# A diffusion backbone block on one core: transform table loaded earlier, value folds and inverse split by parity, filter envelopes on VectorE, more filler matmuls

## The chip, the core and the metric

The kernel runs on one core of a Trainium2 chip. The metric is the time on the device of one launch, in microseconds. A core has TensorE (PE: matmuls, with weight loads PEld beside them), VectorE (DVE), ScalarE (ACT), GpSimd (POOL) and SyncE (SP), which here only issues transfers. Each engine works through its own list in order and waits on semaphores that others raise.

## The reference

Two layers over 1024 latent tokens of width 1024, with 256 context tokens, all in float32. Layer 0 mixes with gated linear attention (GLA) in 4 heads and, in 512 channels, with a bidirectional Hyena convolution; layer 1 mixes with a gated short convolution. Each layer ends in a mixture of experts: top group of 4, then the top 2 of its 8 experts. The change touches the Hyena convolution:

```python
t = jnp.linspace(0.0, 1.0, L)[:, None]
hh = jnp.sin(f2 * (jnp.sin(f1 * (z @ w1 + b1)) @ w2 + b2)) @ w3
window = jnp.exp(-t * jnp.abs(deltas)[None])
hh = hh.reshape(L, 2, HY_WIDTH) * window[:, None]      # h_fwd, h_bwd
U = jnp.fft.rfft(u, n=2*L, axis=1)
K = jnp.fft.rfft(h_fwd, n=2*L, axis=0) + jnp.conj(jnp.fft.rfft(h_bwd, n=2*L, axis=0))
y = jnp.fft.irfft(U * K[None], n=2*L, axis=1)[:, :L]
out = x0 * (y + u * skip)                              # u = v * x1
```

## The kernel before

All of SBUF that is worked on is one arena with tiles laid over each other in time; the eight banks of PSUM are reused likewise. The order of the work on every engine is written out by hand, and waits are counts of semaphores.

**The start.** TensorE makes the modulation vectors from four slabs of weights of 2 MB, then GLA projections and heads; the Hyena projections are put between the heads' steps. `fold` turns finished modulation rows to columns.

**The Hyena part**, in the order of TensorE:
1. `hyena_transposes`: the value tile VX (channels by time) is turned to time by channels in PSUM, and ScalarE copies it into VTM (L965), one half for each parity `par` of time. `vtm_ready` counts the copies. VX is VectorE's product L2022.
2. `residue` (L1386): the values times the transform table DFT, for two groups g of frequencies, four pairs i = (par, fn) each, two banks (s = 0, 1) a pair. ScalarE copies the second bank to USECOND (L974), VectorE writes sum and difference into USUM[g] (L2040, L2043). `butterfly` counts these folds. USUM[1] lies over VTM.
3. Filter rows (L1417): 8 tiles t of filter values for both directions from the hidden layer HH2 (64 partitions) and W3H. ScalarE copies one bank to FTMP (L979); VectorE makes HSUM and HDIF (L2051, L2052), then multiplies HSUM with the envelope WIN (L2056) while GpSimd multiplies HDIF (L715). After every second t come `gate_part` matmuls (L1171), which spread the gates over the partitions, and a `gate_row` copy.
4. `filter_spectrum` (L1396): four blocks kt of the filters' transform, from HSUM and HDIF. For each block VectorE makes sums (L2072, L2073) and complex products with USUM into YF (L2080 to L2089); after each second block four pair additions (L2100) and four pair differences (L2103).
5. `inverse` (L1440): the inverse transform, half g = 0 from the first two blocks and g = 1 from the others; each accumulates `part(c, par, g)` for 4 channel tiles c and 2 parities of time in bank 2c + par. VectorE adds the skip and multiplies with x0 (L2113, L2116).
6. `mix_and_route` (L1473 and on): output projection, residual, norm, router, tables of the experts' rows.

**SyncE's queue** issues in this order: envelope table, (wait: last Hyena projection, hidden filter layer, VX finished) filter hidden layer, W3H, DFT (4 MB, over the projections' input U), (wait: envelope products) IDFT, output weights, x again for the residual (after the inverse's last matmul).

**Experts** take 24 passes of 128 rows in each layer: `turn` transposes gathered rows, `pass_up` twice (L1608), `pass_down` (L1632). The final rows are combined after the last pass has been scattered, and `ov_left` is raised by all five engines before the next part.

**Fillers.** `spare(n, b)` puts n matmuls of constants into a bank that nobody reads:

```python
def spare(n, b):
    for _ in range(n):
        nc.tensor.matmul(bank(b)[:, 0:256], ident, cst[:, 0:256], start=True, stop=True)
```

Each is two instructions at L1115.

## Time and profile before

| what | value |
|---|---|
| runs | 2656.6, 2666.64, 2668.95 us; median 2666.64 |
| profiled execution | 2666.26 us, its span 2664.3 us |
| mean clock granted to TensorE | 0.956 |
| busy, share of the span | PE 92%, PEld 42%, DVE 38%, ACT 12%, POOL 6% |

A start time counts from the begin of the span. An entry such as `564.00 30.53 PE L1386 ... x64 [14.93 <-DMA ...]` is a run of 64 instructions of line 1386 that began at 564.00, ended 30.53 us later, and before which the engine had been idle for 14.93 us until the named transfer landed. A float32 matmul shows as two instructions. A granted clock of 1.00 is 2.4 GHz, 0.50 is 1.2 GHz; a stretch between holds both.

### The profile page before, as it was taken

What the parts mean: (1) busy time and instruction counts of PE and PEld (TensorE: products, weight loads), DVE (VectorE), ACT (ScalarE), POOL (GpSimd) and SP (SyncE); (2) the same over time, 40 slices, a digit from 0 to 9 for tenths busy, and PEclk for the clock granted to TensorE, in tenths of its full rate; (3) what the DMA queues carried; (4) which work ended last, traced back from release to release, by engine and by line L of the source; (5) the groups of instructions that cost most, each with busy time, mean ns of one, the idle gap of its engine ahead of it and who ended that gap; (6) DMA issues with size and microseconds to landing.
All of it is one profiled execution on the core that took longest, in us unless ns stands there. A gap on an engine that the chain in (4) does not pass through costs nothing. (4 is left out here: it accounts for less than half of the span.)

```text
span 2664.3 us, 32938 instructions
## 1 busy us (share of the span) xinstructions
PE 2459.2 (92%) x14399; PEld 1109.7 (42%) x14400; DVE 1018.8 (38%) x2030; ACT 332.4 (12%) x648; POOL 152.8 (6%) x171
## 2 busy tenths in 40 slices
PE   5999998969999899999999799999999999999991
PEld 3455444535555533333333544444555333333330
DVE  2787477726846422222121411011464222222214
ACT  2211233320011100000000410000111000000001
POOL 2000000001000000000000000000000000000000
PEclk9999999986999899999999899999998999999995
DMA  9575001010120799999997701010007999999975
GB/s 338 182 259 196 16 24 30 34 71 32 63 87 32 284 349 397 388 390 395 381 369 304 236 24 47 24 55 32 24 32 294 373 390 384 385 393 383 395 280 214
DMA packets 121869, 572.04 MB, mean 215 GB/s; under 512 B 11744, under 2 KB 48808, under 8 KB 94713
## 3 DMA queue, kind: packets, MB, share of 16 engines
q1 hardware_dynamic: 104328, 526.47, 51.6%
q0 software_dynamic: 17312, 43.16, 4.1%
q8 instruction: 115, 1.88, 0.3%
q10 hardware_dynamic: 80, 0.26, 0.0%
q14 instruction: 34, 0.27, 0.0%
HBM read 548.61 MB, written 38.01 MB: 220 GB/s over the span
## 5 line engine op out<-in xcount | busy, mean ns | idle before, releaser
L1608 PE MATMUL ps<-arena 128*32 128x512 f32 x6144 | 693.2, 604 | 28.5 <-DMA arena<-in_ex_w_dram 27.9
L1608 PEld LDWEIGHTS ps<-arena 128*32 128x32 f32 x6144 | 200.2, 112 | 453.5 <-issue 452.2
L1632 PE MATMUL ps<-arena 128*32 128x512 f32 x3072 | 343.4, 599 | 8.9 <-DMA arena<-in_ex_w_dram 8.8
L1710 PE MATMUL ps<-arena 128*128 128x512 f32 x768 | 330.4, 593 | 4.5 <-ACT arena L1003 4.5
L2315 DVE TENSOR_SCALAR arena<-ps,gain_x,mod 128x128 f32<-128x128 f32 x384 | 126.8, 403 | 373.4 <-PE ps L1593 373.4
L1473 PE MATMUL ps<-arena 128*128 128x512 f32 x512 | 226.6, 597 | 2.9 <-DVE arena L2116 1.6
L1710 PEld LDWEIGHTS ps<-arena 128*128 128x128 f32 x768 | 146.0, 190 | 186.3 <-issue 186.3
L1632 PEld LDWEIGHTS ps<-arena 128*32 128x32 f32 x3072 | 108.4, 111 | 234.7 <-issue 234.7
L2347 DVE SCALAR_TENSOR_TENSOR arena<-ps,arena,gates 128x512 f32<-128x512 f32 x96 | 72.1, 751 | 263.9 <-PE ps L1632 263.9
L1284 PE MATMUL ps<-arena 128*128 128x512 f32 x384 | 167.3, 594 | 0.7 <-issue 0.7
L2323 DVE TENSOR_TENSOR arena<-arena,ps 128x512 f32<-128x512 f32 x48 | 52.6, 1095 | 276.0 <-PE ps L1608 276.0
L1473 PEld LDWEIGHTS ps<-arena 128*128 128x128 f32 x512 | 95.3, 191 | 112.6 <-issue 108.8
L1063 ACT ACTIVATE arena<-ps 128x512 f32<-128x512 f32 x48 | 28.7, 597 | 743.9 <-PE ps L1575 743.9
L2449 DVE TENSOR_TENSOR arena<-arena,ps 128x1024 f32<-128x1024 f32 x8 | 9.8, 1220 | 281.9 <-PE ps L1710 281.9
L1284 PEld LDWEIGHTS ps<-arena 128*128 128x128 f32 x384 | 72.2, 191 | 87.9 <-issue 87.4
L1862 DVE SCALAR_TENSOR_TENSOR arena<-arena,silu_c 128x512 f32<-128x512 f32 x120 | 90.2, 752 | 4.3
L733 POOL DMA_INDIRECT expert_rows<-arena x48 | 48.1, 1001 | 753.0 <-DVE arena L2347 753.0
L1115 PE MATMUL ps<-constants 128*128 128x256 f32 x270 | 73.0, 424 | 0.0
L1061 ACT ACTIVATE arena<-ps 128x512 f32<-128x512 f32 x48 | 28.7, 597 | 351.9 <-PE ps L1608 351.9
L1208 PE MATMUL ps<-arena 128*128 128x512 f32 x160 | 70.1, 595 | 0.0
L723 POOL DMA_INDIRECT arena<-normed_rows,arena x48 | 48.6, 1013 | 371.4 <-PE ps L1593 299.7
L1247 PE MATMUL ps<-arena 128*128 128x512 f32 (+1 forms) x160 | 63.3, 553 | 0.0
(287 smaller groups left out, 2078.8 us busy)
## 6 DMA issues: line engine op xcount, KB each, us to landing
arena<-in_ex_w_dram SPq DMA_DIRECT2D x192, 2048.0 KB, 11.9
arena<-in_mod_w_dram SPq DMA_DIRECT2D x24, 2048.0 KB, 8.7
arena<-expert_rows SPq DMA_DIRECT2D x16, 1024.0 KB, 8.6
arena<-in_od_w_in_dram SPq DMA_DIRECT2D x24, 512.0 KB, 6.4
arena<-in_x_dram SPq DMA_DIRECT2D x2, 4096.0 KB, 15.0
normed_rows<-arena POOLq DMA_DIRECT2D x16, 512.0 KB, 2.9
arena<-in_ev_w_in_dram SPq DMA_DIRECT2D x3, 2048.0 KB, 13.0
arena<-in_ev_w_in_dram SPq DMA_DIRECT2D x12, 512.0 KB, 4.2
```

The source lines that it names most:

```text
L1115: nc.tensor.matmul(bank(b)[:, 0:256], ident, cst[:, 0:256], start=True, stop=True)
L1208: ins = nc.tensor.matmul(bank((2, 3, 6)[i % 3]), u_cols(i, j), w[:, j], start=j == 0, stop=j == KC - 1)
L1247: ins = nc.tensor.matmul(bank(s % 4)[:, 0:n], wqk[:, j, c0:c0 + P], u_part(part, j), start=j == 0, stop=j == KC - 1)
L1284: ins = nc.tensor.matmul(bank(6 + half), HYP[n % 3][:, j], u_part(half, j), start=j == 0, stop=j == KC - 1)
L1473: ins = nc.tensor.matmul(bank(m % 4), mixed[:, j, i * P:(i + 1) * P], slab(first[half], KC, 512)[:, j], start=j == 0, stop=j == KC - 1)
L1608: ins = nc.tensor.matmul(bank(2 + m)[c:c + n], x[:, j, c:c + n], w_slot(e % 2, m, KC, FE)[:, j], start=j == 0, stop=j == KC - 1)
L1632: ins = nc.tensor.matmul(bank(5 + half)[c:c + n], HT[:, j * P + c:j * P + c + n], w_slot(e % 2, 2, FC, D)[:, j, half * 512:(half + 1) * 51 ...
L1710: ins = nc.tensor.matmul(bank(2 * k + half), slab(L1_IN + c, 3, KC, P)[:, k, j], u_part(half, j), start=j == 0, stop=j == KC - 1)
L1862: link(V.scalar_tensor_tensor(out=acc, in0=w[:, j], scalar=silu_c[:, j, 0:1], in1=acc, op0=ALU.mult, op1=ALU.add))
L2315: ins = V.tensor_scalar(XT[:, b, j * P:(j + 1) * P], bank(j // 4)[:, (j % 4) * P:(j % 4 + 1) * P], gain_x[:, 2 * l + 1, j:j + 1], mod[:, l ...
L2323: return V.tensor_tensor(HS.rearrange("t (c p) -> t p c", p=P), SL.rearrange("t (p c) -> t p c", c=FC), bank(3).rearrange("t (p c) -> t p ...
L2347: V.scalar_tensor_tensor(out=YS[:, b, cs], in0=bank(5 + half), scalar=PASS_GATE[:, p:p + 1], in1=gates[:, 1, cs], op0=ALU.mult, op1=ALU.mu ...
```

## The change

- The DFT table's issue moves ahead of the waits for the filter's hidden layer and VX, and of the two filter loads; it waits only for the last Hyena projection.
- The residues' banks are renumbered (2i + s instead of (2i + 4) mod 8 + s), so the filter rows' first banks are those of i = 0 and 1. USUM[1] is laid out so that the folds of i = 0 and 1 fall on the half of VTM for parity 0; they wait for 12 residues instead of 16. The first filter rows wait for 10 and 12 folds instead of 14 and 16.
- GpSimd's eight products of HDIF with the envelope go to VectorE, behind those of HSUM.
- In the inverse the parity becomes the outer loop and the channel tile the inner one. The pair folds are split into those for even and those for odd outputs, and the matmuls of a parity wait only for theirs. The skip and mix follow in the same order.
- Fillers: three more behind each of the first three modulation slabs; two and one more in the tail of each layer's router; nine more ahead of the first expert transposes and six more ahead of the last pass down, in each layer; ten new ones ahead of the short convolution.

```diff
 HSUM, HDIF = at(4096, 2 * KT, HW), at(30720, 2 * KT, HW)
-USUM = [at(0, 8, HW), at(34816, 8, HW)]
+USUM = [at(0, 8, HW), at(34816, 2, 4, HW)]
+
+def usum(g, q):
+    return USUM[1][:, q % 2, q // 2] if g else USUM[0][:, q]
+
 PTMP = [at(20480, 2, HW), at(47104, 2, HW)]
...
     sp.wait_ge(hy_mm, 6 * HC)
+    sp.dma_start(at(12288, 8192), a["dft"]).then_inc(tables_in, 16)
     sp.wait_ge(flt_in, 64)
...
     sp.dma_start(W3H[0:HID], a["hy_w3"][0]).then_inc(flt_in, 16)
-    sp.dma_start(at(12288, 8192), a["dft"]).then_inc(tables_in, 16)
...
     pool.wait_ge(tables_in, 32)
-    for t in range(2 * KT):
-        pool.wait_ge(dif_ready, t + 1)
-        nc.gpsimd.tensor_tensor(HDIF[:, t], HDIF[:, t], WIN[:, t], ALU.mult).then_inc(filt_win, 1)
...
                 act.wait_ge(butterfly, 2 * (i + 1))
-            nc.scalar.activation(USECOND[:, i], bank((2 * i + 4) % 8 + 1), ACT.Copy).then_inc(uk_ready, 1)
+            nc.scalar.activation(USECOND[:, i], bank(2 * i + 1), ACT.Copy).then_inc(uk_ready, 1)
     for t in range(2 * KT):
...
             if n < NMOD - 1:
-                spare(4, 7)
+                spare(7, 7)
             if n == 2:
...
             pe.wait_ge(butterfly, 2 * (i + 1))
-        elif i == 2:
+        elif i == 0:
             pe.wait_ge(omix_ready, 2 * HEADS)
         for tc in (2 * s, 2 * s + 1):
-            ins = nc.tensor.matmul(bank((2 * i + 4) % 8 + s), DFT[:, 2 * g, fn, par, tc * P:(tc + 1) * P], VTM[:, par, tc],
+            ins = nc.tensor.matmul(bank(2 * i + s), DFT[:, 2 * g, fn, par, tc * P:(tc + 1) * P], VTM[:, par, tc],
                                    start=tc == 2 * s, stop=tc == 2 * s + 1)
...
             else:
-                pe.wait_ge(butterfly, 14 + 2 * t)
+                pe.wait_ge(butterfly, 10 + 2 * t)
             for k in range(2):
...
         for g in range(2):
-            pe.wait_ge(butterfly, folds_before(2 * g + 2))
-            for c in range(HC):
-                for par in range(2):
+            for par in range(2):
+                pe.wait_ge(butterfly, folds_before(2 * g + 2) - 4 + 4 * par)
+                for c in range(HC):
                     if g == 0:
...
         turn_rows(TT - 1)
-        spare(4, 2)
+        spare(6, 2)
         places(TT - 2)
-        spare(1, 2)
+        spare(2, 2)
         logits(TT - 1)
...
         table_of_gates(l)
-        spare(2, 2)
+        spare(11, 2)
         turn(0)
...
             turn_hidden(p)
-        spare(12, 0)
+        spare(18, 0)
         pass_down(NP - 1)
...
+        spare(10, 0)
         pe.wait_ge(ov_left, 5)
...
     for g in range(2):
-        u = USUM[g]
         for i, (plus, minus, turned) in enumerate(((0, 4, 0), (2, 6, 1), (1, 7, 0), (3, 5, 0))):
-            dve.wait_ge(dft_mm, 16 if g else 2 * (i + 1))
+            dve.wait_ge(dft_mm, (12 if i < 2 else 16) if g else 2 * (i + 1))
             dve.wait_ge(uk_ready, 4 * g + i + 1)
-            first, second = bank((2 * i + 4) % 8), USECOND[:, i]
-            V.tensor_tensor(u[:, plus], first, second, ALU.add).then_inc(butterfly, 1)
+            first, second = bank(2 * i), USECOND[:, i]
+            V.tensor_tensor(usum(g, plus), first, second, ALU.add).then_inc(butterfly, 1)
             if turned:
                 first, second = second, first
-            V.tensor_tensor(u[:, minus], first, second, ALU.subtract).then_inc(butterfly, 1)
+            V.tensor_tensor(usum(g, minus), first, second, ALU.subtract).then_inc(butterfly, 1)
...
         V.tensor_tensor(HSUM[:, t], HSUM[:, t], WIN[:, t], ALU.mult).then_inc(filt_win, 1)
+        V.tensor_tensor(HDIF[:, t], HDIF[:, t], WIN[:, t], ALU.mult).then_inc(filt_win, 1)
         if t % 2:
...
             for fn in range(2):
-                a, b = USUM[g][:, 4 * half + 2 * fn], USUM[g][:, 4 * half + 2 * fn + 1]
+                a, b = usum(g, 4 * half + 2 * fn), usum(g, 4 * half + 2 * fn + 1)
                 V.tensor_tensor(a, a, b, ALU.add).then_inc(butterfly, 1)
...
         dve.wait_ge(butterfly, folds_before(kt) + 4)
-        u, y = USUM[kt // 2][:, 4 * (kt % 2):4 * (kt % 2) + 4], YF[:, kt]
+        u, y = [usum(kt // 2, 4 * (kt % 2) + q) for q in range(4)], YF[:, kt]
         if kt:
...
             t0, t1 = (PTMP[row // 2][:, q] for q in range(2))
-            step(V.tensor_tensor(y[:, row + 1], u[:, 0], w[:, second], ALU.mult))
-            step(V.tensor_tensor(y[:, row], u[:, 2], w[:, 2 - second], ALU.mult))
-            n = step(V.tensor_tensor(t0, u[:, 1], w[:, second + 1], ALU.mult))
-            step(V.tensor_tensor(t1, u[:, 3], w[:, 3 - second], ALU.mult))
+            step(V.tensor_tensor(y[:, row + 1], u[0], w[:, second], ALU.mult))
+            step(V.tensor_tensor(y[:, row], u[2], w[:, 2 - second], ALU.mult))
+            n = step(V.tensor_tensor(t0, u[1], w[:, second + 1], ALU.mult))
+            step(V.tensor_tensor(t1, u[3], w[:, 3 - second], ALU.mult))
             settle(n)
...
             pairs = ((y[:, 0], z[:, 0], 1), (y[:, 2], z[:, 2], -1), (y[:, 1], z[:, 3], 1), (y[:, 3], z[:, 1], 1))
-            for p, q, sign in pairs:
-                V.tensor_tensor(p, p, q, ALU.add if sign > 0 else ALU.subtract).then_inc(butterfly, 1)
-            for n, (p, q, sign) in enumerate(pairs):
-                dve.wait_ge(butterfly, folds_before(kt) + 4 + n + 1)
-                V.scalar_tensor_tensor(out=q, in0=q, scalar=-2.0 * sign, in1=p, op0=ALU.mult, op1=ALU.add)\
-                    .then_inc(butterfly, 1)
-    for c in range(HC):
-        for par in range(2):
-            n = 2 * c + par
-            dve.wait_ge(idft_mm, n + 1)
+            for m in (0, 2):
+                for p, q, sign in pairs[m:m + 2]:
+                    V.tensor_tensor(p, p, q, ALU.add if sign > 0 else ALU.subtract).then_inc(butterfly, 1)
+                for n, (p, q, sign) in enumerate(pairs[m:m + 2]):
+                    dve.wait_ge(butterfly, folds_before(kt) + 4 + 2 * m + n + 1)
+                    V.scalar_tensor_tensor(out=q, in0=q, scalar=-2.0 * sign, in1=p, op0=ALU.mult, op1=ALU.add)\
+                        .then_inc(butterfly, 1)
+    for par in range(2):
+        for c in range(HC):
+            n, m = 2 * c + par, HC * par + c
+            dve.wait_ge(idft_mm, m + 1)
             sl = slice(par, SEQ - 1 + par, 2)
-            tmp = CTMP[:, n % 2]
-            if c:
-                dve.wait_ge(hmix_ready, n - 1)
+            tmp = CTMP[:, m % 2]
+            if m >= 2:
+                dve.wait_ge(hmix_ready, m - 1)
             link(V.scalar_tensor_tensor(out=tmp, in0=VX[:, c, sl],
```

## Rows read from the trace of the kernel before

**Rows 1.** The page's slices: the clock granted to TensorE, in tenths (40 equal slices).
```profile
PEclk9999999986999899999999899999998999999995
```

**Rows 2.** Timeline of TensorE, Hyena part (start, us, engine, line, operation; in brackets the idle before).
```profile
524.50 1.45 PE L1284 MATMUL ps<-arena 128*128 128x512 f32 x3
...
564.00 30.53 PE L1386 MATMUL ps<-arena 128*128 128x512 f32 x64 [14.93 <-DMA arena<-in_dft_dram]
598.38 7.18 PE L1417 MATMUL ps<-arena 64*128 64x512 f32 x8 [3.86 <-DVE arena L2043]
605.50 3.67 PE L1171 MATMUL ps<-constants,mod 128*128 128x64 f32 x16
...
641.70 56.71 PE L1396 MATMUL ps<-arena 128*128 128x512 f32 x128 [0.29 <-DVE arena L2056]
...
717.79 16.78 PE L1440 MATMUL ps<-arena 128*128 128x256 f32 x64 [5.56 <-DVE arena L2103]
736.13 20.87 PE L1473 MATMUL ps<-arena 128*128 128x512 f32 x48 [1.57 <-DVE arena L2116]
```

**Rows 3.** Timelines of ScalarE and of SyncE's queue, before the transform table lands.
```profile
549.10 0.60 ACT L965 ACTIVATE arena<-ps 128x512 f32<-128x512 f32 x1 [0.26 <-PE ps L1369]
...
548.29 0.58 SPq L609 DMA_DIRECT2D arena<-in_dft_dram  x1
```

**Rows 4.** Stretches: busy us (x instructions) of each engine; near the end TensorE's granted clock.
```profile
564.00:570.00 6.00, 6.00 (x8) 2.59 (x9) 0.00 (x0) 0.00 (x0) 0.00 (x0) 0.53 0.00 0
570.00:594.50 24.50, 24.50 (x58) 10.57 (x56) 5.15 (x8) 4.18 (x7) 0.00 (x0) 1.00 0.00 1
...
598.40:641.40 43.00, 43.00 (x96) 24.07 (x96) 25.87 (x29) 4.78 (x8) 10.60 (x8) 0.50 0.00 0
641.70:645.00 3.30, 3.30 (x4) 1.51 (x5) 3.23 (x6) 0.00 (x0) 0.00 (x0) 0.53 0.72 194
...
717.80:723.40 5.60, 5.60 (x14) 4.50 (x15) 1.44 (x2) 0.00 (x0) 0.00 (x0) 0.51 0.37 138
```

**Rows 5.** Timeline of VectorE in the filter rows: the envelope products of t = 0 and 1.
```profile
604.30 0.69 DVE L2056 TENSOR_TENSOR arena<-arena 128x512 f32<-128x512 f32 x1
...
607.65 1.75 DVE L2056 TENSOR_TENSOR arena<-arena 128x512 f32<-128x512 f32 x1
```

**Rows 6.** Timeline of VectorE during the spectrum and the inverse.
```profile
671.61 0.69 DVE L2072 TENSOR_TENSOR arena<-ps,arena 128x512 f32<-128x512 f32 x1 [1.24 <-ACT arena L985]
...
702.04 0.68 DVE L2073 TENSOR_TENSOR arena<-ps,arena 128x512 f32<-128x512 f32 x1
...
712.83 2.50 DVE L2100 TENSOR_TENSOR arena<-arena 128x512 f32<-128x512 f32 x4
```

**Rows 7.** Timeline of TensorE at the places of the fillers.
```profile
39.49 1.92 PE L1143 MATMUL ps<-arena 128*32 128x512 f32 x16 [0.69 <-DMA arena<-in_mod_w_dram]
...
880.98 1.95 PE L1496 MATMUL ps<-w_router,arena 128*128 128x36 f32 x16 [0.61 <-DVE arena L2192]
...
899.64 2.06 PE L1115 MATMUL ps<-constants 128*128 128x256 f32 x4
904.25 1.97 PE L1593 MATMUL ps<-constants,arena 128*128 128x128 f32 x8 [2.56 <-DMA arena<-normed_rows,arena]
...
1456.93 7.05 PE L1632 MATMUL ps<-arena 128*32 128x512 f32 x64
...
1464.40 5.35 PE L1115 MATMUL ps<-constants 128*128 128x256 f32 x24
1474.01 8.77 PE L1632 MATMUL ps<-arena 128*32 128x512 f32 x64 [4.26 <-DMA arena<-in_ex_w_dram]
1487.97 7.09 PE L1171 MATMUL ps<-constants,mod 128*128 128x64 f32 x32 [5.19 <-POOLq L780]
...
2030.74 2.06 PE L1115 MATMUL ps<-constants 128*128 128x256 f32 x4
...
2601.78 9.85 PE L1632 MATMUL ps<-arena 128*32 128x512 f32 x64 [4.13 <-DMA arena<-in_ex_w_dram]
```

## The prediction

> **What bounds the kernel now.** I read the page's slices first: TensorE is nearly always busy, and its granted clock dips in the slices around 600 and 900 us [rows 1]. Then I read the timeline of TensorE through the Hyena part, looking only at the brackets (what it waited for) [rows 2], the queue entries that explain those waits [rows 3], the clock of the same stretches [rows 4], the VectorE and GpSimd rows inside them [rows 5, 6], and last the places of the filler matmuls [rows 7]. The reader is to see that between 526 and 736 us TensorE is either working or waiting for one named thing, so a wait removed there moves everything behind it. Four waits stand out: 14.93 us for the transform table, 3.86 us for VectorE's last value folds, 5.56 us for its folds before the second half of the inverse, 1.57 us for its mix. There is also a long stretch at the low clock: 43.0 us of the filter rows at 0.50 with TensorE busy all through. The experts behind that part follow TensorE's pace, so I carry shifts through them one to one.
>
> **The table.** It is issued at 548.29 us because it stands in SyncE's queue behind the wait for VX; it lands at 564.00, 15.7 us later. After the change it waits only for the last Hyena projection, which ends at 524.50 + 1.45 = 525.95. It lands near 541.7. Nothing else on SyncE's queue is delayed: the two small filter loads then wait for VX alone and are issued at 547 us as before, long ahead of their use. The next thing that is late is the turned value tile: ScalarE's last copy ends at 549.10 + 0.60 = 549.70 [rows 3]. The first residue needs also the GLA mix, which is over by then. So residues start at 549.8: **-14.2**. If the table still landed last, this would be 0.
>
> **The clock behind it.** After the wait the residues start at 1.2 GHz, and 564.00 to 570.00 is granted 0.53 [rows 4]: about 5.7 us at half clock, a loss of 2.8. With a gap of under 1 us and transposes just before it I expect 1.8 us of loss, **-1.0** (bounds 0 and -2.8).
>
> **Folds by parity.** USUM[1] lies on the value tile, so all its folds now wait for the last residue. By parity the folds of i = 0 and 1 can start after 12 of 16. The filter rows then use banks 0 to 3, which are freed by these, and go on directly behind the residues: the 3.86 us go, **-3.9**. VectorE's remaining four folds (4 x 0.6) end 2.5 us after the last residue. The gates' columns wait for them, but come 3.4 us after it.
>
> **First filter rows at the high clock.** Two rows of t (x8) take 7.18 us at 0.50 [rows 2, 4]. At 1.00 a 512-column instruction takes 24.50 / 58 = 0.42 us, so they would take 3.4. Without the pause the first pair of t starts at the high clock: **-3.7**. The columns for the gates take 3.67 us per 16; their rate hangs on weight loads of 128 columns, so I keep it. I assume the clock then falls, and stays at 0.50 for the other three pairs, since rows of 64 partitions with TensorE fully busy did not raise it once in 43.0 us.
>
> The Trainium skill, "TensorE: Matmul & The Clock Gate", section "Why this matters for your kernels", says that the clock is kept by leaving no idle gaps between bursts of matmuls. By that rule the whole stage would run at 2.4 GHz here, since the gap ahead of it goes; the row at 0.50 with 43.00 us busy in 43.00 speaks against busy time alone deciding it. The sum with the rule would be that of rival A.
>
> **Envelope products on VectorE.** Eight GpSimd products leave and eight come to VectorE. A VectorE product is 0.69 us when it got in first and 1.75 beside a GpSimd product [rows 5]. Per pair of t VectorE now has 2 x (1.4 for sum and difference with its settling + 1.75) + 0.6 = 6.9 us; afterwards 2 x (1.4 + 0.6 + 0.6) + 0.6 = 5.8. TensorE's pair is 7.2 + 3.6 = 10.7, or 7.0 at the high clock, and covers either. The price is 0; with a product still at 1.75 it would be 10.4 per pair, still just under cover. The last product ended 0.3 us behind TensorE: **-0.3**.
>
> The Trainium skill, "SBUF — State Buffer", section "Who interferes with whom", says that VectorE with two SBUF inputs and a GpSimd instruction that reads SBUF exclude each other on a shared port. The 1.75 against 0.69 agrees; by it the new products take the short time, and the sum is the same.
>
> **Transform and inverse.** The spectrum (56.71 us) is unchanged, and from the second block on VectorE sets the pace: its chain from 671.6 to 717.7 us has no idle [rows 6]. So the inverse's second half waits for the pair folds, two runs of four, each 2.50 us, from 712.83 on. Split by parity, even outputs need the first four operations: ready at 712.83 + 2.4 = 715.3 instead of 717.79. A new wait comes ahead: in the first half, c = 2 now follows after 3.5 us (701.9), and its banks are free when VectorE's sums of kt = 3 end, at 702.7: 0.9 us of idle, but it ends 2 us before the second half may start, so it costs nothing. In the second half the low clock (0.51 for 5.6 us, 2.8 lost [rows 4]) may be avoided, since the idle ahead of it shrinks from 5.56 to 2.1. But then VectorE's eight mixes bind: they start at 717.7 behind the odd folds and take 1.73 each, end 731.6; with the low clock kept, 733.5. Against 736.13 that is -4.5 or -2.6; I take **-4.1**. The load of x for the residual follows the inverse's last matmul and moves with it. Should TensorE's first four output parts cover it less, up to 1 us returns.
>
> **Fillers.** One spare costs 5.35 / 12 = 0.45 us at the high clock and 0.87 at the low [rows 7]. Each place by itself:
> Three more behind each of the first three modulation slabs: 9 x 0.45 = 4.0 us, cover 0.69 (the slab of 39.49). The rest pushes the fold and all behind it: **+3.3** (bounds +2.0, if the slab behind the fold then meets a higher clock, and +7.1 at the low clock).
> Two and one more in each router's tail go before gaps that hold them, the narrower 0.61: 0.
> Nine more ahead of the first expert transposes. In layer 0 the tables end at 899.64 and the clock is low there; the gather lands at 904.25. Some five fillers at 0.87 and six at 0.43 end at 906.6, 2.3 late, and 0.9 comes back as the transposes run at the high clock: +1.5. In layer 1 the fillers start at 2030.74 and only two stood before the transposes, with no wait for the gather: fillers end near 2037.1, net +4.0. Together **+5.5** (bounds +1.6, all at the high clock, and +12, all at the low one).
> Six more ahead of the last pass down: the 12 end 4.26 us before the weights land, 6 x 0.45 = 2.7 fits, and the remaining idle is 1.6. Then the pass should run its 64 instructions in 7.05 us as the one before it, not in 8.77 and 9.85: **-4.5** (bound 0).
> Ten more ahead of the short convolution: 4.5 us in a wait of 5.19 for GpSimd: 0; at the low clock +3.5, behind which VectorE's combine, not TensorE, sets the order.
>
> **Sum.** -14.2 - 1.0 - 3.9 - 3.7 - 0.3 - 4.1 = -27.2 in the Hyena part; +3.3 + 5.5 - 4.5 = +4.3 in the fillers; together -22.9. The profiled execution took 2666.3 us (2664.3 of span and 2.0 around it), and the median of the runs shown is 2666.6, so both give the same: **2643.4 us**.
>
> **The rivals.**
> A, the filter rows keep 2.4 GHz, from the first pair to the last. Three more pairs at 7.0 instead of 10.7 are -11.1, and the spectrum starts without 3.3 us at 0.53, -1.6: 2630.7 us. For it: nothing idles ahead of them any more. Against it: the 43.0 us at 0.50 [rows 4]. It is what the rule of the Trainium skill named above would give.
> B, the fillers are exposed. All added fillers are 9 + 6 + 18 + 12 + 10 = 55, at 0.45 us 24.7: that eats the gain, and at 0.87 (47.9) the kernel would end at 2666.3 - 27.2 + 47.9 = 2687 us. It turns slower once over 31 of the 55 run at the low clock outside any wait. For it: the clock is at 0.50 at 900 and at 2031. Against it: the 5.19 and 4.26 us waits hold 22 of them.
> C, half exposed: the upper bounds of the modulation and table terms (+7.1 and +12) with no gain in the last passes: -27.2 + 19.1 = -8.1, 2658 us.
> D, the table was not what the residues waited for, or they meet another wait of 10 us or more (the folds' banks): -14.2 and -1.0 fall away, 2658.6 us. Against it: the bracket names the table, and both other producers end by 549.7.
>
> **How the numbers follow.** Forecast 0.68, A 0.13, B 0.03, C 0.10, D 0.06. The forecast's own bounds are 2634 (clock terms best: -1.8, -0.4, -3.9 in the tables, -1.3) and 2653. Leaving out B, most of C and D, the range is 2630 to 2653. A measurement of this kernel tells about 0.5% from no change, 13.3 us, so the line is 2653.3: faster 0.88 (forecast, A, a share of C and D), within 0.5% 0.09, slower 0.03.
>
> **What would show it.** Residues starting within 1 us of ScalarE's last value copy; no gap between residues and filter rows; the VectorE product at 0.6 to 0.7; granted clock of the filter stage 0.50 after its first pair (A: 1.00); the inverse's second half starting 2.5 us after the pair folds begin; the transposes after the tables' fillers later by 2 and 4.5 us; last passes near 7.05. Wrong would make it chiefly the clock of the filter stage, and fillers at a low clock.

## The result and the profile after

| | before | after |
|---|---|---|
| runs | median 2663.23 us (2656.6 to 2668.95, 4 runs) | median 2623.45 us (2622.0 to 2628.67, 4 runs) |
| profiled execution | span 2664.3 us | 2623.91 us, span 2622.1 us |
| mean granted clock | 0.956 | 0.977 |

The ratio is 0.9855, with a 95% interval from 0.9826 to 0.9884: the change makes the kernel faster by 31 to 46 us. The forecast was 2643.4 us with a range from 2630 to 2653. The sign was right; the gain is larger than the range allowed.

The page's slices of the clock after, which answer to [rows 1]:

```profile
PEclk9999999989999999999999999999998999999996
```

The 8 and 6 at the ninth and tenth slice (533 to 666 us) have become an 8 and a 9. The timeline of TensorE through the Hyena part after, which answers to [rows 2] (start, us, engine, line, operation; in brackets the idle before):

```profile
552.03 1.98 PE L1370 MATMUL ps<-constants,arena 128*128 128x128 f32 x8 [3.53 <-DVE arena L2024]
554.69 30.80 PE L1387 MATMUL ps<-arena 128*128 128x512 f32 x64 [0.69 <-ACT arena L966]
585.43 3.82 PE L1418 MATMUL ps<-arena 64*128 64x512 f32 x8
589.18 2.00 PE L1172 MATMUL ps<-constants,mod 128*128 128x64 f32 x16
591.10 3.82 PE L1418 MATMUL ps<-arena 64*128 64x512 f32 x8
...
611.20 56.90 PE L1397 MATMUL ps<-arena 128*128 128x512 f32 x128 [3.00 <-DVE arena L2058]
667.94 3.62 PE L1441 MATMUL ps<-arena 128*128 128x256 f32 x16
672.46 10.63 PE L1441 MATMUL ps<-arena 128*128 128x256 f32 x48 [0.91 <-DVE arena L2075]
685.07 14.08 PE L1441 MATMUL ps<-arena 128*128 128x256 f32 x64 [1.98 <-DVE arena L2106]
700.72 20.87 PE L1474 MATMUL ps<-arena 128*128 128x512 f32 x48 [1.57 <-DVE arena L2119]
```

The clock of the same stretches, which answers to [rows 4] (busy us and instructions of TensorE, granted clock, share of the DMA engines, GB/s):

```profile
555.00:561.00 6.00, 6.00 (x8) 0.51 0.08 16
561.00:585.40 24.40, 24.40 (x58) 1.00 0.00 1
585.50:608.10 22.60, 22.60 (x96) 1.00 0.00 1
608.10:611.20 3.10, 0.11 (x1) 1.00 0.00 0
611.30:614.30 3.00, 3.00 (x5) 0.63 0.78 191
```

The bracket ahead of the residues is 0.69 instead of 14.93 and names ScalarE's copy instead of the table. The table is issued at 530.89 and lands 13.5 us later, some ten us before the first residue. There is no bracket ahead of the filter rows. And the filter stage (from the first filter row to the spectrum), 43 us at 0.50 before, runs at 1.00: eight instructions of filter rows (four matmuls) take 3.82 us instead of 7.18, and sixteen of the gate columns take 2.00 instead of 3.67. VectorE is now what ends the stage, with 3.00 us of idle ahead of the spectrum.

VectorE after, at the end of the filter rows, which answers to [rows 5]:

```profile
601.37 0.69 DVE L2057 TENSOR_TENSOR arena<-arena 128x512 f32<-128x512 f32 x1
601.98 0.69 DVE L2058 TENSOR_TENSOR arena<-arena 128x512 f32<-128x512 f32 x1
...
610.46 0.69 DVE L2058 TENSOR_TENSOR arena<-arena 128x512 f32<-128x512 f32 x1
```

Every product takes 0.68 or 0.69, none 1.75. From 588.25 on VectorE runs without a wait for another engine; a pair of tiles t comes each 5.85 us (from the copy of L1896 at 599.36 to the one at 605.21).

The filler places after, which answer to [rows 7]:

```profile
57.52 3.65 PE L1184 MATMUL ps<-constants,arena 128*128 128x128 f32 x16
62.15 1.97 PE L1184 MATMUL ps<-constants,arena 128*128 128x128 f32 x8 [0.98 <-DVE arena L1793]
63.91 8.06 PE L1209 MATMUL ps<-arena 128*128 128x512 f32 x16
...
864.01 7.01 PE L1116 MATMUL ps<-constants 128*128 128x256 f32 x22
870.86 1.04 PE L1594 MATMUL ps<-constants,arena 128*128 128x128 f32 x8
...
1476.37 10.15 PE L1712 MATMUL ps<-arena 128*128 128x512 f32 x16 [1.45 <-issue]
...
1991.04 6.68 PE L1116 MATMUL ps<-constants 128*128 128x256 f32 x22
```

Where the time went, from marks of the two profiles on TensorE (each row is the change of one stage's length, and they add up to the shift of TensorE's last instruction):

| stage | forecast | measured |
|---|---|---|
| modulation and first transposes | +3.3 | +2.9 to the first transpose, +2.0 behind it |
| bracket ahead of the residues | -14.2 | -14.2 |
| residues (their slow start), bracket behind them | -1.0, -3.9 | +0.3, -3.9 |
| first filter row to spectrum (43.32, now 25.77 us) | -3.7, -0.3 | -17.5 |
| spectrum | 0 | +0.2 |
| inverse up to the output projection (37.88, now 32.78) | -4.1 | -5.1 |
| then to the first pass of layer 0 | +1.5 | +1.0 |
| experts of layer 0 (573.73, now 564.23) | half of -4.5 | -9.5 |
| then to the first pass of layer 1 (554.27, now 562.47) | +4.0 | +8.2 |
| experts of layer 1 (574.58, now 568.25) | half of -4.5 | -6.3 |
| sum | -22.9 | -42.1 |

The rows are rounded; the last is the shift itself. Two places hold the miss of 19.2: the filter stage (13.5 more gain than forecast) and the experts (11.3 more). The layer 1 part and the modulation give 5.8 of it back.

### The profile page after: what moved, and what is told of

It is laid out like the page before. It is cut to its first block and busy times, and to the rows that moved or that the text cites. A ratio compares the mean times of both kernels' runs of the same rounds, so it can differ in the third digit from the quotient of the medians.

```text
span 2622.1 us, 33157 instructions
## 1 busy us (share of the span) xinstructions
PE 2443.3 (93%) x14509; PEld 1113.0 (42%) x14510; DVE 1015.7 (39%) x2038; ACT 332.5 (13%) x648; POOL 142.2 (5%) x163
## 5 line engine op out<-in xcount | busy, mean ns | idle before, releaser
L1609 PE MATMUL ps<-arena 128*32 128x512 f32 x6144 | 680.4, 595 | 26.3 <-DMA arena<-in_ex_w_dram 25.1
L1633 PE MATMUL ps<-arena 128*32 128x512 f32 x3072 | 338.9, 592 | 8.0 <-DMA arena<-in_ex_w_dram 8.0
L1116 PE MATMUL ps<-constants 128*128 128x256 f32 x380 | 95.3, 406 | 0.0
L1116 PEld LDWEIGHTS ps<-constants 128*128 128x128 f32 x380 | 75.4, 205 | 15.0 <-issue 4.7
## 6 DMA issues: line engine op xcount, KB each, us to landing
arena<-in_x_dram SPq DMA_DIRECT2D x2, 4096.0 KB, 14.9
```

The costliest lines, as they stand in the source:

```text
L1609: ins = nc.tensor.matmul(bank(2 + m)[c:c + n], x[:, j, c:c + n], w_slot(e % 2, m, KC, FE)[:, j], start=j == 0, stop=j == KC - 1)
L1633: ins = nc.tensor.matmul(bank(5 + half)[c:c + n], HT[:, j * P + c:j * P + c + n], w_slot(e % 2, 2, FC, D)[:, j, half * 512:(half + 1) * 51 ...
```

## Experiments

Single executions of one kernel here differ by up to 1% (the kernel before took 2644.8 to 2669.9 us over 24 runs beside the first four experiments), so medians tell parts of 4 us barely, and a stage's length in the profiles tells them well. Each ratio is to the kernel before, run on the same chip. Comments behind `#` in the edits are added for the reader, and `...` stands for lines left out.

**The table alone.** The kernel before with its table load moved up, nothing else:

```
+    sp.dma_start(at(12288, 8192), a["dft"]).then_inc(tables_in, 16)    # ahead of the wait for VX
...
-    sp.dma_start(at(12288, 8192), a["dft"]).then_inc(tables_in, 16)
```

> The kernel before with one edit: the transform table is issued right after the last Hyena projection. Theory G (the idle stretch ahead of the filter rows lets the clock fall, and once low these rows do not raise it): residues start within 1 us of ScalarE's last value copy, 14.2 us earlier; the 3.9 us of idle ahead of the filter rows stay, and the stage from the first filter row to the spectrum stays at a granted clock of 0.50 and near 43 us. Total about -14 us. Theory S (what matters is the earlier start, or chance): the clock of the stage is 1.00 and the stage some 27 us here too, total about -30 us.

Measured: 2652.08 us, ratio 0.9964 (0.9943 to 0.9985), a gain of 10 us (4 to 15) where 14 were expected. TensorE in the profile of this kernel:

```profile
550.74 29.30 PE L1386 MATMUL ps<-arena 128*128 128x512 f32 x64 [0.69 <-ACT arena L965]
583.90 6.69 PE L1417 MATMUL ps<-arena 64*128 64x512 f32 x8 [3.87 <-DVE arena L2043]
```

The bracket of 14.93 has become 0.69, as in the full change. The filter rows are as slow as before, although they start 14.5 us earlier, and the stage takes 42.8 us.

**The folds in the old order.** The changed kernel, with the folds waiting for all sixteen residues again and the filter rows for all folds:

```
-                    dve.wait_ge(dft_mm, (12 if i < 2 else 16) if g else 2 * (i + 1))
+                    dve.wait_ge(dft_mm, 16 if g else 2 * (i + 1))
...
-                        pe.wait_ge(butterfly, 10 + 2 * t)
+                        pe.wait_ge(butterfly, 16)
```

> The changed kernel, but the filter rows wait for all 16 value folds, and the second group's folds wait for all residues, as in the kernel before. Theory G: about 3.9 us of idle return ahead of the filter rows, the clock falls and stays at 0.50 through the stage, which goes from 25.8 us to 43: about +21 us against the changed kernel, near 2645. Theory P (the products leaving GpSimd, or the banks, keep the clock high): the stage stays at 1.00 and near 26 us, +4 us only.

Measured: 2652.15 us, ratio 0.9967 (0.9947 to 0.9988). TensorE in its profile:

```profile
588.83 7.18 PE L1418 MATMUL ps<-arena 64*128 64x512 f32 x8 [5.06 <-DVE arena L2044]
```

With the gap back, the low clock is back, for 42.9 us, although the products are all on VectorE and the table is early. Here the clock falls while TensorE idles in the gap:

```profile
583.90:585.50 1.60, 0.00 (x0) 1.00 0.00 0
585.50:587.00 1.50, 0.00 (x0) 0.79 0.00 0
587.00:588.70 1.70, 0.00 (x0) 0.50 0.00 0
```

**The same gap, filled.** As the last kernel, and nine fillers in the gap:

```
+                pe.wait_ge(uk_ready, 5)
+                spare(9, 1)
                 pe.wait_ge(flt_in, 96)
```

> The kernel with the late folds, and nine filler matmuls on constants in the stretch where TensorE would idle ahead of the filter rows (9 x 0.45 = 4.0 us). Theory G: the wait stays, but TensorE does not idle in it, so the clock stays at 1.00 and the stage near 26 us: about +4 us against the changed kernel, near 2628. If the late folds themselves or something behind them lowered the clock, the stage is at 0.50 here too, +21 us.

Measured: 2633.31 us, ratio 0.9909 (0.9879 to 0.994). TensorE in its profile:

```profile
582.54 4.05 PE L1116 MATMUL ps<-constants 128*128 128x256 f32 x18
587.76 3.79 PE L1420 MATMUL ps<-arena 64*128 64x512 f32 x8 [1.17 <-DVE arena L2046]
591.48 2.00 PE L1172 MATMUL ps<-constants,mod 128*128 128x64 f32 x16
```

The folds are as late as before, the filter rows start 5.05 us behind the residues' end (5.06 in the last kernel), and the stage takes 25.75 us. Between this kernel and the last, only matmuls that compute nothing, and the wait ahead of them, differ. In these two profiles the idle ahead of the stage is what costs 17 us. The medians are less tidy: by the ratios the last kernel lies 30 us above the changed one and this one 14 us, where 21 and 4 were expected. The nine executions of this kernel spread from 2620.5 to 2650.8 us, and the profile is that of the fastest. The three slowest (2638.3 to 2650.8 us) have a mean granted clock of 0.966 to 0.970, nearly that of the kernel with the open gap (0.964 to 0.968), the other six 0.975 to 0.978. Whether the 1.17 us of idle that is left lets the clock of the stage fall in some executions is not shown.

**A shorter gap.** The changed kernel, with VectorE's folds by parity kept and only TensorE's wait set back, so that the gap is about half as long:

```
-                        pe.wait_ge(butterfly, 10 + 2 * t)
+                        pe.wait_ge(butterfly, 16)
```

> The changed kernel in which the filter rows of TensorE wait for all sixteen folds, while VectorE still makes them in the order by parity, so that TensorE idles some 2 to 2.5 us ahead of the filter rows, half of the gap of the kernel with the folds in the old order (5.06 us). Theory G (an idle gap ahead of the filter rows is what drops the clock): if a gap of half the length is enough, the filter rows come at 7.2 us per four and the stage takes about 43 us; the whole is some 19 us above the changed kernel. Theory T (the drop needs the longer gap): the stage stays at 3.8 us per four and takes some 26 us, and only the 2 to 2.5 us of the gap is lost.

Measured: 2642.09 us, ratio 0.9931 (0.9906 to 0.9955). TensorE's timeline and, below, its clock in stretches, in the profile of this kernel:

```profile
586.63 5.62 PE L1418 MATMUL ps<-arena 64*128 64x512 f32 x8 [2.67 <-DVE arena L2044]
592.18 3.67 PE L1172 MATMUL ps<-constants,mod 128*128 128x64 f32 x16
```

```profile
577.00:583.00 6.00, 6.00 (x16) 1.00 0.00 0
583.90:586.60 2.70, 0.06 (x1) 1.00 0.00 0
586.70:592.10 5.40, 5.40 (x8) 0.66 0.00 0
592.00:627.00 35.00, 35.00 (x85) 0.50 0.00 0
```

2.67 us of idle are enough. The clock is still 1.00 during the gap, falls within the first eight instructions of filter rows, and then stays at 0.50 to the end of the stage (41.3 us). Here the fall comes behind the idle; in the gap of 5.06 us above it came inside. Either way the bracket to look at is the one ahead of the slow stretch.

**The gap of the kernel before, filled.** The kernel before and nothing of the change, with nine fillers:

```
                 pe.wait_ge(omix_ready, 2 * HEADS)
+                pe.wait_ge(uk_ready, 5)
+                spare(9, 5)
```

> The kernel before with one edit: nine fillers in the idle time of 3.86 us ahead of the filter rows, in a bank that the residues no longer use; table, folds, products on GpSimd and VectorE, inverse and all other fillers as before. Theory G (the idle gap alone decides the clock of the filter stage): the filter rows come at 3.8 us per four tiles, the gate columns at 2.0 per sixteen, and the stage from the first filter row to the spectrum falls from 43 to between 26 and 29 us; with the products of HSUM on GpSimd it is bound there (28.4 in the changed kernel with these products), so some 14 to 17 us less in all, 2644 to 2648. Theory S (the stage is fast only when the table, the folds by parity or an earlier start are there too): 43 us again and no change, 2660.

Measured: 2645.18 us, ratio 0.9934 (0.9914 to 0.9954). TensorE in its profile:

```profile
592.67 4.05 PE L1115 MATMUL ps<-constants 128*128 128x256 f32 x18
596.65 3.82 PE L1419 MATMUL ps<-arena 64*128 64x512 f32 x8
...
616.44 2.59 PE L1419 MATMUL ps<-arena 64*128 64x512 f32 x4 [0.66 <-DVEq L2057]
618.97 3.67 PE L1171 MATMUL ps<-constants,mod 128*128 128x64 f32 x16
625.07 56.72 PE L1396 MATMUL ps<-arena 128*128 128x512 f32 x128 [2.43 <-DVE arena L2058]
```

The stage takes 28.4 us instead of 43.3: two lines of code give 15 us of the stage, and 18 us (12 to 23) of the whole by the ratio. It is 2.6 longer than the changed kernel's 25.8, because VectorE's products beside GpSimd's now bind. In the last pair of tiles the clock falls once more, behind a wait of 0.66 us.

**The products.** The changed kernel with the products of HDIF on GpSimd again:

```
+            for t in range(2 * KT):
+                pool.wait_ge(dif_ready, t + 1)
+                nc.gpsimd.tensor_tensor(HDIF[:, t], HDIF[:, t], WIN[:, t], ALU.mult).then_inc(filt_win, 1)
...
-                V.tensor_tensor(HDIF[:, t], HDIF[:, t], WIN[:, t], ALU.mult).then_inc(filt_win, 1)
```

> The changed kernel, but GpSimd multiplies HDIF with the envelope again. In the changed kernel VectorE and TensorE take 5.85 and 5.7 us for a pair of filter tiles at the high clock, so VectorE is no longer covered. Theory V (the product beside GpSimd's costs 1.75 us): VectorE needs 2 x (1.4 + 1.75) + 0.6 = 6.9 us per pair, four pairs 27.6 instead of 23.4: +4 us. Theory N (the move does not matter, as forecast for a stage covered by TensorE at the low clock): within 1 us. If the idle of TensorE that this opens in every pair lets the clock fall: +17 us.

Measured: 2627.11 us, ratio 0.9887 (0.9844 to 0.9931); the ratio alone does not tell it from the changed kernel. In its profile VectorE's product takes 1.76 us beside GpSimd's, and TensorE waits for it:

```profile
612.40 57.68 PE L1400 MATMUL ps<-arena 128*128 128x512 f32 x128 [1.21 <-DVE arena L2060]
```

From the first filter row to the spectrum it is 28.42 us, where the changed kernel has 25.77. Here too the last pair falls to 0.50, behind a wait of 0.67 us. The edit is worth 2.6 us at the high clock, and needs the high clock to be worth anything: at 0.50 a pair on TensorE takes 10.7 us and covers either.

**The inverse.** The changed kernel with the inverse's loops and the last folds in the order of before (channel outside, parity inside, one wait for all eight folds). TensorE's lines are shown; VectorE's folds and mixes go back to the same order:

```
-                    for par in range(2):
-                        pe.wait_ge(butterfly, folds_before(2 * g + 2) - 4 + 4 * par)
-                        for c in range(HC):
+                    pe.wait_ge(butterfly, folds_before(2 * g + 2))
+                    for c in range(HC):
+                        for par in range(2):
```

> The changed kernel with the inverse and its folds in the order of the kernel before: channel outside, output parity inside, one wait for all eight folds of the last inverse frequency tile. All else as changed, so that the filter stage and the spectrum should be the same as in the changed kernel. Theory I (the inverse's term of the sum, -4.1 forecast and -4.9 read between the two kernels): from the end of the spectrum to the out projection this kernel takes 4 to 5.5 us more than the changed kernel, with one stall of some 5 us behind the last folds on VectorE, and some 4 to 5 us more in all. Theory C (the inverse gained only because the clock was higher behind the faster filter stage): 0 to 1.5 us more.

Measured: 2626.96 us, ratio 0.9881 (0.9853 to 0.9909). TensorE in its profile:

```profile
668.40 13.98 PE L1441 MATMUL ps<-arena 128*128 128x256 f32 x64
687.92 15.84 PE L1441 MATMUL ps<-arena 128*128 128x256 f32 x64 [5.54 <-DVE arena L2105]
```

36.93 us from the first inverse matmul to the output projection, against 32.78 in the changed kernel: 4.15 us, the term of the sum (4.1). The stall of 5.54 comes back, and the second half takes 15.84 instead of 14.08 behind it.

**The fillers.** The changed kernel with all filler counts of before, and the kernel before with all filler counts of after (the same lines the other way round):

```
-                        spare(7, 7)          # modulation
+                        spare(4, 7)
-                spare(6, 2)                  # router tail
+                spare(4, 2)
-                spare(2, 2)                  # router tail
+                spare(1, 2)
-                spare(11, 2)                 # behind the table of gates
+                spare(2, 2)
-                spare(18, 0)                 # ahead of the last pass down
+                spare(12, 0)
-                spare(10, 0)                 # ahead of the short convolution
```

> The changed kernel with every filler matmul count of the kernel before put back (modulation 4, router tails 4 and 1, table of gates 2, last pass 12, none in the turn of the rows); table, folds, products and inverse stay as changed. Theory N (the counts move only their own places): the span from the start to the residues is 3 to 5 us shorter than in the changed kernel, the two first passes of the experts start together 5 to 6 us earlier, the two last passes take some 2 us more each where the rows wait for fewer fillers or none at all, and the whole is 4 to 9 us below the changed kernel, some 2616. Theory V (the fillers buy the clock): the granted clock falls below 1.00 at the places where counts went down, and the whole is the same or above the changed kernel. Theory F (the counts are what freed the experts' stages of their stretches at 0.83 to 0.91): the 20 us stretches below 1.00 behind waits for weights come back in this kernel, and the experts of the first layer take again some 8 us more than in the changed kernel.

> The kernel before with the changed kernel's filler counts alone (modulation 7, router tails 6 and 2, table of gates 11, last pass 18, 10 ahead of the short convolution); table, folds, products and inverse as before. Theory N (each count moves only its own place): modulation +5, the stage between the tables of gates and the first passes +1 and +4, the two last passes -2 and -3, so +5 in all, some 2665 beside 2660. Theory F (the counts also free the experts' stages of their stretches below 1.00, where the changed kernel took 7.8 and 3.6 us less): the experts of the first layer take 564 to 566 instead of 573.7 us from the first pass to the last, and the whole is 5 to 8 below the kernel before. Theory H (those stretches come by chance, or with the place of a stage in time): the experts of the first layer take anything from 564 to 574, with some stretches at 0.91, and the whole lies between.

Measured: with the old counts in the changed kernel 2620.16 us, ratio 0.9842 (0.9815 to 0.9869); with the new counts in the kernel before 2664.27 us, ratio 1.0007 (0.999 to 1.0024). The counts as a whole cost some 2 to 4 us, or nothing that can be measured (forecast +4.3). By places, in the profile with the old counts: the span up to the residues is 5.1 us shorter than in the changed kernel, the stretch from the first filler behind the tables of gates to the first pass 0.8 us in layer 0 and 3.8 us in layer 1, and the last passes are again 8.77 and 8.55 us instead of 7.07. The filter stage takes 25.76 us, and with the new counts alone in the kernel before it takes 42.05: it owes nothing to the other fillers.

**The kernel before, profiled again.** The experts' 9.5 and 6.3 us had only half an explanation, so the unchanged kernel was profiled a second time.

> The kernel before, unchanged, profiled a second time. Theory H (the stretches at 0.91 in the experts' stages come by chance): their number and place differ from the first profile, where the first layer's experts took 573.7 us from the first pass to the last, and the stage may take some us less. Theory P (they belong to the program): the same stretches, and 573 to 575 us. The filter stage takes 43 us at 0.50 again, and the stages of Hyena agree within 0.5 us.

Measured: 2665.85 us. Stretches of 20 us with a mean granted clock below 0.985 between the passes of layer 0: five in the first profile, one in this. The experts of layer 0 took 571.1 us in it (573.7 in the first), those of layer 1 576.2 (574.6). One such place, in the first profile of the kernel before, first as a row of the timeline and then as stretches:

```profile
981.82 8.77 PE L1608 MATMUL ps<-arena 128*32 128x512 f32 x64 [2.72 <-DMA arena<-in_ex_w_dram]
```

```profile
980.00:984.00 4.00, 2.18 (x16) 0.84 1.02 435
984.00:988.00 4.00, 4.00 (x32) 0.74 1.03 431
988.00:992.00 4.00, 4.00 (x43) 1.00 0.76 245
```

A pass's weights come 2.72 us late with the DMA engines full, and the pass behind that idle takes 8.77 instead of 7.1 us: it looks like what happens to the filter stage, except that these matmuls of 128 rows are back at 1.00 within one pass. Which passes meet it differs from profile to profile. Over all profiles with 12 fillers ahead of the last pass the experts of layer 0 took 573.7, 571.1, 574.4, 569.5 and 566.2 us; over those with 18, 564.2, 568.1, 564.3, 565.7, 565.6, 570.7, 567.7, 566.5 and 568.1. The means are 571.0 and 566.8.

**Two candidates.** The first takes the fillers away where they only delay, and puts some where TensorE idles ahead of long matmuls:

```
-                        spare(7, 7)
+                        spare(4, 7)
...
+            pe.wait_ge(vtm_ready, 4)         # ahead of the last Hyena transposes
+            spare(7, 4)
...
+                pe.wait_ge(mod_gate, 1)      # ahead of the transform
+                spare(6, 4)
...
-                spare(11, 2)
+                spare(4 if l else 6, 2)
...
-                    if i < 4:
-                        spare(4, 0)
+                    spare(4 if i < 4 else 3, 0)
```

> A candidate that takes the readings further. The changed kernel with the modulation's fillers back at 4, the table of gates' fillers at 6 in the first layer and 4 in the second, 3 fillers behind the fifth turn of the rows in the short convolution, and fillers of width 7x and 6x placed in two short idle times, ahead of the last group of Hyena's transposes and ahead of the transform. Theory G (fillers belong only where TensorE would be idle ahead of matmuls that then run long at the low clock): modulation -5, the two tables' fillers -4, the residue's ramp -1.5 to -3, the short convolution -3, so 10 to 14 us below the changed kernel, some 2611. Theory N (fillers that are placed late only delay): no change of the clock behind them, only modulation and tables gain, 8 us in all, and each new group costs 0.5 to 1 us: some 2617.

The second leaves out the group ahead of the last transposes and the three of the short convolution:

> What of the candidate with filled gaps paid, alone: the changed kernel with the modulation's fillers at 4, the table of gates' fillers at 6 in the first layer and 4 in the second, and six fillers in the idle time ahead of the transform. The group ahead of the last transposes is left out again: it took 6.1 us and saved 1.5 us of the residue's ramp. From the profiles of the parts: modulation -5, tables of gates -3, spectrum -2 to -3, so 9 to 11 below the changed kernel, 4 below the candidate with filled gaps, some 2615. If fillers ahead of the transform only delay it, the spectrum takes 57 us and the whole is 2618.

Measured: 2619.89 us, ratio 0.9849 (0.9822 to 0.9875), and 2609.43 us, ratio 0.9814 (0.9794 to 0.9834). For the first 10 to 14 us below the changed kernel were expected; by the ratios it is 2, which can't be told from nothing. Its group ahead of the transposes was a miss, as its timeline shows:

```profile
546.88 6.14 PE L1116 MATMUL ps<-constants 128*128 128x256 f32 x14 [3.13 <-ACT arena L966]
552.86 1.11 PE L1370 MATMUL ps<-constants,arena 128*128 128x128 f32 x8
554.67 27.73 PE L1389 MATMUL ps<-arena 128*128 128x512 f32 x64 [0.70 <-ACT arena L966]
```

It came at the end of the idle instead of in it and ran at the low clock itself: 6.14 us, for 1.6 us in the residues (27.73, against 29.30 with the old filler counts and 29.43 in the second candidate). From the first transposes to the residues this kernel takes 499.9 us, the second candidate 495.4. The group ahead of the transform pays in both; the second candidate's timeline:

```profile
603.01 2.81 PE L1116 MATMUL ps<-constants 128*128 128x256 f32 x12
606.16 55.20 PE L1397 MATMUL ps<-arena 128*128 128x512 f32 x128 [0.35 <-DVE arena L2060]
```

The spectrum takes 55.20 us in both, instead of 56.90 in the changed kernel (56.9 to 58.3 in the four profiles with 3.0 us of idle ahead of it), and starts no later. The second candidate is the fastest kernel made here: by its ratio 49 us (44 to 55) below the kernel before. Its interval and that of the changed kernel just overlap, so that it also beats the changed kernel is likely, not certain.

## Why the prediction was wrong

**The step that failed** stands under "First filter rows at the high clock": "I assume the clock then falls, and stays at 0.50 for the other three pairs". It does not fall. The 43 us at 0.50 were read as a property of the rows of 64 partitions. They were the effect of what stood ahead of them: this stage didn't climb from the low clock in up to 43 us, and didn't fall from the high one in the 22.8 us that TensorE works in it, as long as nothing idled inside (with waits of 0.66 and 0.67 us ahead of its last rows, the last pair fell). The evidence for that reading, TensorE fully busy at 0.50, was true, and says only the first half. With a gap of 5.06 or 2.67 us the stage takes 42.9 and 41.3 us; with the gap filled, 25.75; in the kernel before with the gap filled, 28.4. This is rival A, at 0.13. The Trainium skill, "TensorE: Matmul & The Clock Gate", section "Why this matters for your kernels", says the same: idle gaps between bursts of matmuls are to be avoided, because the throughput drops with them. The trace agrees: 42.9 us behind the gap, 25.75 with it filled. Rival A's 2630.7 us still lay 7 above the result; its 1.6 us in the spectrum did not come, since 3.00 us of idle now stand ahead of it and its first 3 us are granted 0.63.

**A second error inside it**: the gate columns' rate "hangs on weight loads of 128 columns, so I keep it". The loads do fill the time (3.49 us of the 3.67 per sixteen instructions before, 1.83 of 1.90 after), but they follow the clock as well: 3.67 us at 0.50, 2.00 at 1.00. So TensorE's pair of tiles is 5.7 us, not the 7.0 that rival A reckoned with.

**The products' cover** went with it. "TensorE's pair ... covers either" held for 10.7 and 7.0, not for 5.7 against VectorE's 5.85. VectorE binds, and the stage ends with 3.00 us of idle. The price of the products was forecast well (5.8 per pair), and the edit is worth 2.6 us instead of the 0.3 in the sum. The Trainium skill's rule on the shared port ("SBUF — State Buffer", section "Who interferes with whom") states that the two exclude each other, and the rows agree: 0.69 alone, 1.76 beside a GpSimd product; and where VectorE got in first, at 604.30 in the kernel before, GpSimd's took 1.76 instead of 1.26.

**Right by place and size**: the table (-14.2 forecast; the bracket shrinks by 14.2 both alone and in the change), the gap behind the residues (-3.9, -3.9), the inverse (-4.1; 5.1 between the profiles, 4.15 when it alone is undone), the tables of gates (+1.5 and +4.0; from the first filler to the first pass it is +1.2 and +4.0).

**The ramp of the residues**, -1.0, can't be told from chance: the residues take 30.53 us in the first profile of the kernel before and 29.23 in the second, 30.80 in the changed kernel, and 29.1 to 30.8 in those of its experiments that have no fillers ahead of the last transposes. The clock is low at their start in all, here behind the bracket of 3.53 ahead of those transposes.

**The modulation's fillers**: +3.3 forecast, +2.9 up to the first transposes. The other 2.0 of the table lie behind them: the eight transposes at 62.15 take 1.97 us instead of 1.09, and the first value matmuls 8.06 instead of 7.03. From the first transposes to the residues three of the six kernels with seven fillers (the changed one, the shorter gap, the inverse by channel) take 497.2 to 497.4 us, the others 495.1 to 495.5, and the three with four and an early table whose transposes have no fillers ahead 495.4 to 495.8. So 3 us is the fillers' price, and the 2 comes and goes.

**The last passes**: -4.5 forecast. From the first filler to the end of the pass it is 18.38 before and 16.63 after in layer 0, 19.32 and 17.40 in layer 1, so -3.7. The pass itself falls to 7.07 as forecast, but in layer 1 the weights land 10.3 us behind the first filler instead of 9.5. Nor do 18 fillers secure the 7.07: with them the shorter gap and the inverse by channel have a last pass of 8.64 and 8.77 us in layer 1, behind 2.35 and 2.88 us of idle, and the changed kernel one of 7.07 behind 2.40. Both last passes take 7.1 us in seven of the nine profiles with 18 fillers.

**The rest of the experts** (-12.1 beyond the last passes) was in no term. Part of it seems to be chance: the kernel before showed five such stretches in one profile and one in another, and the changed kernel's profile is among the luckiest of those with its experts' code. The two means differ by 4.2 us, of which 1.8 is the last pass; whether the rest is more than chance is not shown. **In layer 1**, 3.0 of the unforecast 4.2 us is one group of matmuls at 1476.37 that took 10.15 instead of 7.11 us. It took 8.6 to 10.2 in six of the fourteen profiles and 7.1 in the others; five of nine with the ten fillers ahead of the short convolution are slow, and one of five without. It comes and goes, and whether the fillers favour it stays open.

**The lower bound** was also added up wrongly: the terms named beside 2634 give -7.4, so 2636. The result lies below this as well as below the 2630 of the range.

So of the 19.2 us by which the profile missed the forecast, 13.5 lies in the filter stage: 11.2 is its clock (28.4 us with the products on GpSimd, 14.9 below the 43.3 of before, of which 3.7 was forecast), and 2.3 the products, which pay only at the high clock. The experts' 11.3 is open in the main, and the rest is sizes.

## What to carry to other kernels

When a stage runs at the low clock with TensorE fully busy, look at the bracket ahead of it before you call the clock a property of the stage. A gap's price is its own length and what it does to the stage behind it: 1.7 us for 3.00 us of idle ahead of 128-row matmuls, 15 to 17 us for 2.67 to 5.06 ahead of 64-row ones. In this kernel fillers paid only inside such a gap; where nothing idled they cost their full time, and at the end of a gap they ran slowly themselves. And when a forecast says that one engine covers another, work out the cover again at the speed that a rival gives.

## What of the hardware was not expected

- The same instructions, with TensorE busy all through, stay at either clock: 35.00 us busy of 35.00 at 0.50 with a gap ahead of them, 22.60 of 22.60 at 1.00 without. Matmuls of 128 partitions and 512 columns climb back from there in 6 us (555.00 to 561.00 at 0.51 in the changed kernel, then 1.00), in other profiles in some 3 (with the gap filled: 0.74 over 555.00 to 558.00, then 1.00).
- The fall can come after the idle: in the kernel with the shorter gap the granted clock is 1.00 during the 2.70 us and 0.66 over the next 5.40. In the kernel with the folds in the old order it is 0.79 and then 0.50 inside the gap of 5.06 us.
- Late in a stage that VectorE binds, less is enough: in the kernel before with its gap filled, one wait of 0.66 us is followed by a group at 3.67 instead of 2.00, and in the kernel with the products on GpSimd one of 0.67 us by 0.50 over the next 3.80. Yet in the profile with the gap filled, 1.17 us of idle ahead of the stage left the clock at 1.00. So the length of an idle alone does not tell whether the clock falls; what else decides it is not shown.
- Sixteen instructions (eight matmuls) of 64 columns, each with weights of 128x128, take 3.67 us at the low clock and 2.00 at the high: close to the ratio of the clocks. Their time is mostly not columns: at the 0.42 us of a 512-column instruction, 64 columns would be some 0.05 of their 0.125 us each (an estimate), and the weight loads are busy for 1.83 of 1.90 us.
